# Identity products in TensorE's idle places, and one weight split cut into quarters inside the attention

## What is computed

```
for l in range(2):
    h = rms_norm(x, norm_mix_pre[l])
    m = even_mixer(h) if l == 0 else nsa(h)   # retention + spatial gating | sparse attention
    x = x + rms_norm(m, norm_mix_post[l])
    h = rms_norm(x, norm_ffn_pre[l])
    f = (gelu(conv3(h @ f_w_in[l]).a) * conv3(h @ f_w_in[l]).b) @ f_w_out[l]
    x = x + rms_norm(f, norm_ffn_post[l])
```

## Time and profile before

| | us |
|---|---|
| median of 3 runs | 1611.31 (1610.95 to 1613.89) |
| the profiled execution | 1613.73 |
| its span, first to last instruction | 1612.0 |
| PE busy | 1567.7 (97% of the span) |
| DVE busy | 836.5 (52%) |
| ACT busy | 690.7 (43%) |
| POOL busy | 229.9 (14%) |
| mean granted clock of TensorE | 0.99 of full speed |

### The profile page before, as it was taken

One profiled execution on the slowest core, in us unless ns is written; L12 is line 12 of the kernel. 1 busy time (PEld: TensorE's weight loads), 2 busy tenths in 40 slices (PEclk: granted clock), 3 DMA queues, 4 the chain that ended last, 5 costly groups with the idle time before them and its releaser, 6 DMA issues.

```text
span 1612.0 us, 29956 instructions
## 1 busy us (share of the span) xinstructions
PE 1567.7 (97%) x12323; PEld 1401.0 (87%) x12323; DVE 836.5 (52%) x1359; ACT 690.7 (43%) x1311; POOL 229.9 (14%) x574
## 2 busy tenths in 40 slices
PE   8999999999999999998999999999989999999998
PEld 7799989699999999996677566667989999999997
DVE  4855452655532555568234676743585552355523
ACT  5222134555532545432323565655545552355522
POOL 3000001300000000002013444422020000000001
PEclk9999999999999999999999899999999999999999
DMA  7322337023233332322344400033203324233231
GB/s 229 101 81 81 100 80 188 17 83 101 62 95 96 86 97 62 95 70 80 114 132 92 150 9 2 1 119 78 79 27 92 90 60 116 79 96 87 63 86 56
DMA packets 180274, 138.38 MB, mean 86 GB/s; under 512 B 11408, under 2 KB 164272, under 8 KB 180112
## 3 DMA queue, kind: packets, MB, share of 16 engines
q1 hardware_dynamic: 172288, 113.26, 24.4%
q0 software_dynamic: 7888, 23.79, 5.1%
HBM read 128.21 MB, written 13.01 MB: 88 GB/s over the span
## 4 chain that ended last, share of the span: by engine, by line
PE 89%; DVE 6%; ACT 2%; issue 1%; POOL 1%; DMA 0%; POOLq 0%; ACTq 0%; DVEq 0%
PE gemm L1150 42%; PE gemm L714 18%; PE gemm L725 9%; PE misc L683 6%; PE gemm L1290 3%; PE misc L1321 2%; PE misc L888 1%; DVE hL L1909 1%; PE misc L1426 1%; PE gemm L888 1%; PE misc L761 1%; DVE y L1983 1%; DVE y L1969 1%; PE misc L844 1%; PE misc L1315 0%
## 5 line engine op out<-in xcount | busy, mean ns | idle before, releaser
L1898 DVE TENSOR_TENSOR wL<-raw,wH 128x2048 fp32r<-128x2048 f32 (+1 forms) x106 | 219.6, 2072 | 151.0 <-ACT wH L1460 150.8
L1150 PE MATMUL gemm<-hH,wH 128*128 128x272 f32 x1280 | 268.5, 291 | 0.2
L1150 PE MATMUL gemm<-hH,wL 128*128 128x272 f32 x1280 | 264.8, 288 | 0.0
L1150 PE MATMUL gemm<-hL,wH 128*128 128x272 f32 x1280 | 264.0, 288 | 0.0
L1460 ACT ACTIVATE wH<-raw 128x2048 fp32r<-128x2048 f32 (+2 forms) x110 | 185.9, 1690 | 74.0 <-PE gemm L725 37.5
L1150 PEld LDWEIGHTS gemm<-hH,wH 128*128 128x128 f32 x1280 | 200.6, 188 | 6.1 <-issue 4.1
L1150 PEld LDWEIGHTS gemm<-hL,wH 128*128 128x128 f32 x1280 | 201.1, 188 | 0.0
L1150 PEld LDWEIGHTS gemm<-hH,wL 128*128 128x128 f32 x1280 | 199.9, 189 | 0.0
L2262 DVE SCALAR_TENSOR_TENSOR conv<-up,rows_t,conv 128x560 f32<-128x560 f32 x88 | 70.6, 802 | 208.2 <-ACT conv L1460 208.2
L1460 ACT ACTIVATE up<-gemm 128x32 f32<-128x32 f32 (+2 forms) x264 | 66.0, 324 | 175.0 <-PE gemm L1150 153.7
L714 PE MATMUL gemm<-hH,wH 128*128 128x272 f32 (+1 forms) x624 | 132.6, 294 | 0.9 <-issue 0.6
(11 more groups left out here) (416 smaller groups left out, 2725.5 us busy)
## 6 DMA issues: line engine op xcount, KB each, us to landing
raw<-in_f_w_in SPq DMA_DIRECT2D x88, 512.0 KB, 4.9
raw<-in_f_w_out SPq DMA_DIRECT2D x32, 704.0 KB, 4.6
raw<-in_e_w_in SPq DMA_DIRECT2D x12, 1024.0 KB, 5.1
raw<-in_o_w_in SPq DMA_DIRECT2D x10, 1024.0 KB, 5.1
raw<-in_e_w_out SPq DMA_DIRECT2D x4, 1024.0 KB, 6.1
raw<-in_o_w_out SPq DMA_DIRECT2D x16, 256.0 KB, 6.7
pages<-in_cache_cmp POOLq DMA_DIRECT2D x10, 256.0 KB, 4.1
xin<-in_x_prompt SPq DMA_DIRECT2D x4, 512.0 KB, 6.5
```

Source lines behind the costliest of these rows:

```text
L1150: ins = pe.matmul(gemm[odd][:, n, 0:TH], w, x[:, k, n * TH:(n + 1) * TH], start=(k == 0 and part == 0), stop=(k == nk - 1 and part == 2))
L1898: order(dve.tensor_tensor(unit_view(wL, u), unit_view(raw, u), unit_view(wH, u).bitcast(F32), ALU.subtract), lo_ready)
```

## The change

Seven edits; products and data are the same otherwise.

```diff
 token_unit, u == O_IN + 1 (after sample_products)
                     for k in ks:
+                        if k == 4:
+                            pe.wait_ge(total_ready, TOTALS_AFTER + 1)
+                            stay_busy(10, b7)
                         pe.wait_ge(h_ready, DC * 3 + k + 1)
 first_pair
                 for k in range(DC):
+                    if k:
+                        stay_busy(5, b4)
                     pe.wait_ge(h_ready, DC * fill + k + 1)
 expanded_norms (PE)
                 spread_rstd(n + 1)
-                stay_busy(10, idle)
+                stay_busy(42, idle)
 mix_tokens
+                stay_busy(14, b6)
                 pe.wait_ge(svn_ready, 1)
 gate_weights
                     turn(b7[:, g * P:(g + 1) * P], sgw[:, g, :], gate_turned if g == 3 else None)
+                stay_busy(5, b6)
                 pe.wait_ge(gate_ready, 1)
 loop over the first 12 units
+                if n == 1:
+                    pe.wait_ge(h_ready, DC)
+                    stay_busy(9, b5)
                 if n:
                     unit(u)
 loop over the heads
             for h in range(RH):
+                if h >= 2:
+                    stay_busy(4, gemm[last % 2][:, 1, :])
                 pe.wait_ge(hsq, h + 1)
 DVE, new: a quarter of split_lo
+            def lo_quarter(u, q, sem_):
+                cols = slice(512 * q, 512 * q + 512)
+                dve.wait_ge(hi_ready, u + 1)
+                order(dve.tensor_tensor(wL[:, u % 2, cols], raw[:, u % 2, cols], wH[:, u % 2, cols].bitcast(F32), ALU.subtract), sem_)
 DVE, attention
-                elif n == 16:
-                    split_lo(O_OUT)
+                elif n in (13, 15, 17, 19):
+                    lo_quarter(O_OUT, (n - 13) // 2, lo_ready if n == 19 else None)
```

## The result

| | before | after |
|---|---|---|
| median of 8 runs each, us | 1611.69 | 1620.39 |
| ratio of the times, 95% interval | | 1.005 (1.0036 to 1.0064) |
| the profiled execution, us | 1613.73 | 1618.64 |
| its span, us | 1612.0 | 1616.8 |
| mean granted clock of TensorE | 0.990 | 0.997 |

A forecast was written before the change was run, and what follows sets the result against it. PE was taken to bound the kernel (89% of the chain). The terms summed to +4.25 us, 1618.0 for the profiled execution; the median, 1618.0 or 1615.6, was put at the middle, 1616.8, range 1612.0 to 1621.0.

The forecast's parts named there:

- the sum: All places' terms added for an execution like the profiled one: +4.25 us, or 1618.0 us.
- The second feed-forward's start: 42 and seven times five products overfill the waits up to first_pair's end: 6.3 us later, nothing behind absorbing it.
- the upper end of 7.1: Second feed-forward's start: 7.1 us instead of 6.3 if each change between the two sorts of products costs 0.1 us.
- The second input unit: Nine products, 2.0 us of work in a wait of 1.34 us, with the clock already full: +0.6 us.
- Gate and mixing: Five products at the gate cost +0.2 us; fourteen ahead of mixing remove the low stretch at 91: -1.7 us.
- -2.8: Lower end at the mixing: the last three tiles at full clock with no delay ahead.
- The heads: Four and four products end the sums 0.1 us later; the 24 products behind run at full clock: -1.0 us.
- The attention's input: The 42 cost 0; ten ahead of chunk 4 cost 2.23 us and remove a low stretch worth 1.65: +0.55.
- The quarters: Attention: splitting in quarters removes PE's wait of 1.87 us for POOL and costs 1.2 us: -0.7 us.
- The question left open: Whether low stretches put the profiled execution 2.4 us above the median: 1618.0 us if so, 1615.6 otherwise.
- That identity products don't hold the clock: Rival: low stretches at mixing, heads and chunk 4 stay, added products come on top; 6.95 us more, 1623.8; chance 0.12.
- The other rival, a clock that rises sooner at 900: At the attention's start the low stretch vanishes, at most 4.8 us back: 1612.0 us, not slower; chance 0.18.

The follow-up runs named there:

- the one with the filling taken back: The changed kernel with 10 identity products ahead of the second feed-forward again and none between first_pair's chunks; 1613.37 us, ratio 1.0006.
- the late 42 alone: The kernel before with 42 instead of 10 identity products ahead of the second feed-forward, none in first_pair; 1614.35 us, ratio 1.0012.
- one instead of five: The kernel before with one identity product, not five, ahead of each of seven chunks in first_pair; 1614.1 us in one execution.
- the first four experiments: In the text's order: second feed-forward's filling taken back (1613.37 us), only that filling added to before (1619.36), its fives only (1617.96), its 42 only (1614.35).
- the kernel with the fives alone: The kernel before with only 5 identity products before each of seven chunks in first_pair; 1617.96 us, ratio 1.003.
- the last kernel above: The kernel with what fits, plus five products in gate_weights and fourteen ahead of mix_tokens; 1608.47 us, ratio 0.9976.
- the kernel with what fits: The kernel before with only 42 products at the attention's input (without the ten), the heads' four and four, and the quarters; 1607.7 us, ratio 0.9976.

## Why the prediction was right, and where it wasn't

The forecast of a slower kernel held, and 1620.39 lies in its range, near the upper end; 1616.8 was 3.6 us too low. From profiled execution to profiled execution the sum said +4.25 and the measurement +4.9, but only because errors of both signs met, some of them no effect of the change: 1.6 us more at 790 and some 0.7 less in the attention come with low stretches that change from execution to execution (below), and 0.5 us less each at the start and in the first feed-forward stand where no edit is.

**The second feed-forward's start (6.3 foreseen, 6.33 measured).** The step that decided, and right in each part: no wait left, 29.2 us instead of the foreseen 29.1, nothing given back in the 395.5 us behind. The products cost what was foreseen: 42 last 9.30 us (0.221 each), and five between two chunks add 2.62 - 1.50 = 1.12 us (0.224 each; 1.50 is a chunk of 12 products without a wait). So the changes between the two sorts of products cost nothing, for which the upper end of 7.1 had taken 0.1 us each.

**The second input unit (0.6 foreseen, 0.65 measured).** Right: the stage is 5.99 and 5.95 us in the two kernels that have the nine, and 5.34 or 5.35 in the ten others.

**Gate and mixing (+0.2 - 1.7 foreseen, -0.97 measured, some -0.2 in most executions).** The step that failed is that the low stretch at 91 belongs to this place. It stands there in two of the eight executions without these products; in the six others the same wait of 1.80 us left the clock alone and it fell at 141 to 180. The value that the usual execution allows is the -0.2, taken over both stages. The 1.3 us that the products cost there are what the prediction's own terms give (0.2, and 1.1 between its -2.8 and -1.7).

**The heads (-1.0 foreseen, -0.47 measured).** Mechanism right: the low stretch stands at 214 to 217 in all eight profiled executions without these products and in none of the four with them. Mis-sized was the end of the sums, which come 0.57 us later, not 0.1: the waits of 0.54 and 0.65 us each got 0.89 us of work, and the delay at the second wait adds to that at the first (0.35 + 0.24). In two kernels without the products the low stretch was twice as long (10.28 and 10.42 us for the stage), and there they would be worth 1.7 to 1.9.

**The attention's input (0 and +0.55 foreseen, +0.71 measured).** The size is right, the reason isn't. That the 42 push PE's work to the right, and that this shortens the wait for `xsO`, was foreseen (0.45 measured, 1.3 said); but in the two kernels with the 42 and without the ten this alone held the clock, and the ten only cost (2.2 us). I gave the gain to the wrong edit.

**The quarters (-0.7 foreseen, about -0.8 measured).** Right in sum, by the comparison at 6.8 us: -1.15 in the attention, +0.33 behind it, which I hadn't seen.

**The low stretch at 790 (not foreseen, +1.6).** Work there is as before, as the rows of before and of after show:

```profile
791.20 0.47 PE L725 MATMUL gemm<-wH,hH 128*128 128x512 f32 x1 [2.26 <-issue]
```
```profile
789.78 0.74 PE L725 MATMUL gemm<-wH,hH 128*128 128x512 f32 x1 [2.25 <-issue]
```

The same wait, and the clock falls in four of the twelve profiled executions (after, the one with the filling taken back, the late 42 alone, one instead of five), with no edit that these four share and the others lack. Two of the four, the late 42 alone and one instead of five, are up to 1170 us the same program as before and two others that don't have it. So it comes and goes without any edit, and the 1.6 us in after's execution are no sign of the change; whether the change makes it likelier, one execution can't tell.

**The median.** The profiled execution of before was 2.4 us above the median shown. The question left open, whether low stretches were the reason, has an answer for a part: its mean clock, 0.990, is that of the 35 executions of before that ran beside the first four experiments (median 0.990), so that it hadn't more of them, but one lay where it costs more: 133.47 instead of some 132.4 us from the gate to the retention's end. The profiled execution of after, in turn, lies 1.75 us under its median. The median thus had less to gain than the sum took; with the terms of the usual execution, 6.3 + 0.65 - 0.2 - 0.5 - 0.8 and between 0.7 and 2.25 + 1.6 at the attention's input and behind it, the change costs 6.2 to 9.3 us, and 8 was measured.

**The rivals.** That identity products don't hold the clock is refuted at the heads, the mixing and the second feed-forward's start. There the three kernels with the 42 have no low stretch and the nine with ten products have one (0.50 us for the first pair behind the 42 in after, 0.79 behind a wait of 4.12 us in the kernel with the fives alone). The Trainium skill (TensorE: Matmul & The Clock Gate, Part 4) says that transposes in transpose mode don't count as busy in the same way; for ordinary products against the identity, as here, the traces show no such exception. The other rival, a clock that rises sooner at 900, came in part: 6.8 instead of 10.2 us at the low level in after's profile, worth some 0.7 us (180.61 against 179.77 to 179.93, all without the quarters). It isn't the change's doing, since the same program up to there has 6.8, 10.2 and 13.6.

## What to carry to other kernels

What of the filler doesn't fit into its wait delays the end unless a later wait takes the delay up, so count it wait by wait: seven times five products among waits of 0.2 to 0.9 us cost 5.8 us, while 42 at one wait of 4 us, ahead of work that another engine paces, began that work 2.8 us late and cost nothing. A low stretch is worth removing only where TensorE, not its supplier, sets the end (from the first spread ahead of the attention's input to the second sample products, which wait for `xsO`, all twelve executions took 27.2 us, with 0, 3.4 or 6.8 us at the low level in them); and before a gain is claimed from one, look in a second execution whether it stands in the same place. An edit that only removes a low stretch at the price of equally long filler (the mixing: 1.5 for 1.3 us) brings nothing that can be measured.

## What the runs showed of the hardware that was not expected

**A low stretch has no fixed price.** Read from the stages, one of 6.8 us cost 2.6 us at the mixing and after (17.07 and 116.40 against 14.77 and 116.06) and 2.3 to 2.5 at the heads (what the products brought and the 0.57 that they cost). One of 3.4 us cost 1.5 in the retention, 1.0 to 1.2 at the heads, 1.55 behind `xsO`, 1.4 to 1.6 at 790, and 0 at the start of the second feed-forward. There, in the last kernel above, 6.8 us at the low level, begun before the products, cost no more than 3.4 us (24.08 and 24.10 us for the stage), since each chunk waits for DVE anyway.

**The clock falls where no idle time stands.** In the kernel with what fits, PE in order of time:

```profile
157.46 0.40 PE L987 MATMUL misc<-inner_s,vN 32*128 32x32 f32 x2
157.80 1.95 PE L990 MATMUL misc<-qds,s 128*128 128x4 f32 x16
159.60 0.63 PE L714 MATMUL gemm<-hH,wH 128*128 128x272 f32 x2
```

PE counts as busy for 9.00 of the 9.00 us from 150, but what it does ahead of the fall are products of four columns. In all six executions with a low stretch between 141 and 180 the clock falls within 0.7 us of the end of such a row of sixteen; the retention has four of these rows, and only one of them is followed by a fall. With the mixing's products some 65 us earlier the same rows ran at the full clock and the pair behind them took 0.51 us; none of the four kernels with these products has a low stretch in the retention: filler acts far from its place, by a way that no run here shows.

**The places change from execution to execution.** Five executions are of one program up to 1170 us; their low stretch ahead of the heads stands at 91, 91, 160, 161 and 180, the one at 790 in two of them, and at the attention's start they have 6.8, 10.2 or 13.6 us at the low level. The Trainium skill (TensorE: Matmul & The Clock Gate, Part 1) says that the number of slow products differs from run to run of the same kernel; these executions agree, and show that not only their number but the place changes, with an effect of 1.6 us for one stretch, as large as what most of the edits were to bring.
